# Two transformer blocks on one core: 32 copies of the bias rows, an earlier first weight split, and GpSimd's modulation units moved into the first mixer

## Time and profile before

| what | us |
|---|---|
| median of three runs (lowest, highest) | 928.85 (928.48, 933.09) |
| time of the profiled execution | 928.37 |
| its span, first to last instruction | 926.5 |
| PE busy | 864.4 (93%) |
| DVE busy | 593.9 (64%) |
| ACT busy | 481.2 (52%) |
| POOL busy | 306.3 (33%) |

### The profile page before, as it was taken

One profiled execution on the slowest core, in us unless ns is written; L12 is line 12 of the kernel. 1 busy time (PEld: TensorE's weight loads), 2 busy tenths in 40 slices (PEclk: granted clock), 3 DMA queues, 4 the chain that ended last, 5 costly groups with the idle time before them and its releaser, 6 DMA issues.

```text
span 926.5 us, 16135 instructions
## 1 busy us (share of the span) xinstructions
PE 864.4 (93%) x6742; PEld 836.8 (90%) x6742; DVE 593.9 (64%) x793; ACT 481.2 (52%) x740; POOL 306.3 (33%) x239
## 2 busy tenths in 40 slices
PE   4999999999799997969997979898999999999998
PEld 3899999988799997959997979898999999999998
DVE  4786454347789988586877685655556655546552
ACT  5755545444645653455342524433666666766641
POOL 1100000000699998646876755020153300000000
PEclk8999999999899999979998999999899999999999
DMA  7343597624456675425754454485355545343350
GB/s 258 122 157 132 58 156 164 139 78 174 162 197 227 259 255 211 175 110 205 272 203 155 188 204 160 137 280 182 115 219 192 195 138 182 129 145 137 137 204 23
DMA packets 28247, 158.42 MB, mean 171 GB/s; under 512 B 3456, under 2 KB 3984, under 8 KB 13840
## 3 DMA queue, kind: packets, MB, share of 16 engines
q1 hardware_dynamic: 24816, 146.37, 43.8%
q0 software_dynamic: 3360, 11.03, 7.4%
HBM read 150.04 MB, written 7.34 MB: 170 GB/s over the span
## 4 chain that ended last, share of the span: by engine, by line
PE 80%; DVE 10%; POOL 3%; ACT 3%; issue 2%; DMA 2%; SPq 0%; DVEq 0%; ACTq 0%; POOLq 0%
PE ps L451 78%; DVE wlo L1241 3%; PE ps L637 1%; ACT whi L879 1%; DMA arena<-positions 1%; PE ps L729 1%; DVE olo L1286 1%; DVE arena L1273 1%; DVE arena L1574 1%; DMA raw<-weights 1%; ACT L868 1%; DMA x<-x_t 1%; DVE hlo L1269 1%; POOL ada_ring L376 1%; DVE ohi L1284 0%
## 5 line engine op out<-in xcount | busy, mean ns | idle before, releaser
L1241 DVE TENSOR_TENSOR wlo<-raw,whi 128x1024 fp32r<-128x1024 f32 x224 | 316.1, 1451 | 155.1 <-ACT whi L879 155.1
L451 PE MATMUL ps<-hhi,whi 128*128 128x256 f32 x960 | 284.1, 296 | 32.1 <-DVE wlo L1241 15.6
L451 PE MATMUL ps<-hlo,whi 128*128 128x256 f32 x960 | 276.0, 288 | 0.0
L451 PE MATMUL ps<-hhi,wlo 128*128 128x256 f32 x960 | 275.8, 287 | 0.0
L879 ACT ACTIVATE whi<-raw 128x1024 fp32r<-128x1024 f32 x224 | 225.9, 1052 | 90.3 <-PE ps L451 68.9
L451 PEld LDWEIGHTS ps<-hhi,whi 128*128 128x128 f32 x960 | 188.7, 197 | 37.1 <-issue 36.5
L451 PEld LDWEIGHTS ps<-hlo,whi 128*128 128x128 f32 x960 | 189.0, 197 | 2.0 <-issue 1.9
L451 PEld LDWEIGHTS ps<-hhi,wlo 128*128 128x128 f32 x960 | 188.6, 196 | 0.0
L451 PE MATMUL ps<-ohi,whi 128*128 128x256 f32 x512 | 149.8, 293 | 12.6 <-DVE olo L1286 7.3
L376 POOL TENSOR_TENSOR ada_ring<-ada_ring,sil 128x1024 f32<-128x1024 f32 x48 | 105.7, 2201 | 140.4 <-DMA ada_ring<-ada 140.2
L451 PE MATMUL ps<-ohi,wlo 128*128 128x256 f32 x512 | 147.4, 288 | 0.0
(11 more groups left out here) (195 smaller groups left out, 1038.7 us busy)
## 6 DMA issues: line engine op xcount, KB each, us to landing
raw<-weights SPq DMA_DIRECT2D x112, 1024.0 KB, 5.1
ada_ring<-ada SPq DMA_DIRECT2D x48, 512.0 KB, 5.8
bias_rows_d<-ada_ring POOLq DMA_DIRECT2D x1, 4096.0 KB, 45.8
bias_rows_b<-fb POOLq DMA_DIRECT2D x1, 2048.0 KB, 88.5
arena<-bias_rows_d POOLq DMA_DIRECT2D x2, 1024.0 KB, 9.3
x<-x_t SPq DMA_DIRECT2D x2, 512.0 KB, 4.7
arena<-bias_rows_b POOLq DMA_DIRECT2D x1, 1024.0 KB, 7.4
arena<-bias_rows_d POOLq DMA_DIRECT2D x2, 512.0 KB, 13.1
```

The lines of the kernel that those rows point to most:

```text
L451: return pe.matmul(o, l, r, start=start, stop=stop, skip_group_check=skip)
L1241: dve.tensor_tensor(wlo[:, unit % UNITS, :, :], raw[:, c % RAW, 4 * half:4 * half + 4, :], whi[:, unit % UNITS, :, :].bitcast(F32), ALU.su ...
```

## The change

It has five parts.

1. `scr_d` and `scr_b` get 32 copies of a row instead of 128. They are read back in four DMAs of 32 partitions for each of two column ranges: eight instead of two for layer B, eight instead of four for layer D. `fb` and `fd` move out of their own tile and the ring into `early`, whose memory is later that of `ohi`; DVE therefore waits for the two writes before the norm of layer A's output.
2. At the start ACT calls `high(0)` before it works on the norm's sums, not after it. DVE splits the first half of chunk 0 before it waits for the norm and the second half after the third tile of the input, where both halves came after the first tile.
3. POOL runs the units 0 to 5 when the eight q and k convolutions are done, then the two bias writes, then the units 6 to 29. The loads of layer B's bias and the rope angles follow. The units 30 to 41 wait until layer B's inputs are ready (`h_ok_sem` 24), and 42 to 47 stay where they were. `ada_sum` holds 12 units.
4. SP loads the units 0 and 1 with chunk 11, 2 to 4 with chunk 12, three with each chunk from 13 to 19 (5 to 25), and one with each from 20 to 35 (26 to 41).
5. PE takes six units in each of the levels 2, 4 and 6 (through a turn of the banks 6 and 7), the units 18 to 23 after job 17, 24 to 29 after job 19, 30 to 35 after the jobs 28 to 33, 36 to 38 after job 35, and 39 to 41 after job 37. DVE takes the sums with `mod_of_slot` in the levels and with `take_mod` after that.

The diff, cut to what the prediction speaks of:

```diff
-        ada_sum = sb("ada_sum", [P, 6, P])
+        ada_sum = sb("ada_sum", [P, 12, P])
...
-        fb = sb("fb", [16, 512])
+        fb = early[0:16, 512:1024]
...
-        fd = ring[0:16, 0, 0:4, :].rearrange("p a b -> p (a b)")
+        fd = early[0:16, 0:512]
...
-                    if c == (JOB_B + 1 + u if u < 18 else JOB_C + (u - 18) if u < 42 else 76 + 2 * (u - 42)):
-                        if u < 2:
-                            sp.wait_ge(o_split_sem, 4)
-                            sp.wait_ge(scr_out_sem, 32)
-                        else:
+                    if c == ((11, 11, 12, 12, 12)[u] if u < 5 else 13 + (u - 5) // 3 if u < 26 else u - 6 if u < 42 else 76 + 2 * (u - 42)):
+                        if u >= 2:
                             sp.wait_ge(ada_mul_sem, u - 1)
...
+            pool.wait_ge(sil_ok_sem, 1)
+            pool.wait_ge(conv_ok_sem, 8)
+            for u in range(6):
+                ada_unit(u)
             pool.wait_ge(fd_ok_sem, 2)
             pool.wait_ge(nt_ok_sem, 4)
-            pool.dma_start(scr_d.rearrange("p h t -> h p t"), fd[:, :].unsqueeze(1).to_broadcast([16, P, 512])).then_inc(scr_out_sem, 16)
+            pool.dma_start(scr_d[0:32].rearrange("p h t -> h p t"), fd[:, :].unsqueeze(1).to_broadcast([16, 32, 512])).then_inc(scr_out_sem, 16)
             pool.wait_ge(bias_sb_sem, 1)
-            pool.dma_start(scr_b.rearrange("p h t -> h p t"), fb[0:8, :].unsqueeze(1).to_broadcast([8, P, 512])).then_inc(scr_out_sem, 16)
+            pool.dma_start(scr_b[0:32].rearrange("p h t -> h p t"), fb[0:8, :].unsqueeze(1).to_broadcast([8, 32, 512])).then_inc(scr_out_sem, 16)
+            for u in range(6, 30):
+                ada_unit(u)
             pool.wait_ge(scr_out_sem, 32)
             pool.wait_ge(o_split_sem, 4)
             bias_b = A(bias_at, 8, 384)
...
+            for a in range(0, P, 32):
+                pool.dma_start(bias_b[a:a + 32, :, 0:256], bass.AP(scr_b.tensor, 127 - a, [[8 * 512 - 1, 32], [512, 8], [1, 256]])).then_inc(bias_ok_sem, 16)
+                pool.dma_start(bias_b[a:a + 32, :, 256:384], bass.AP(scr_b.tensor, 255 - a, [[8 * 512 - 1, 32], [512, 8], [1, 128]])).then_inc(bias_ok_sem, 16)
...
-            pool.wait_ge(sil_ok_sem, 1)
-            for u in range(42):
+            pool.wait_ge(h_ok_sem, 24)
+            for u in range(30, 42):
                 ada_unit(u)
...
+                if lv in (2, 4, 6):
+
+                    b = taken(slot_of_mod(lv // 2 - 1))
+                    for u in range(3 * lv - 6, 3 * lv):
+                        ada(u, b)
                 parts(J, 0, 4)
...
             for J in range(JOB_OUT_A, JOB_B):
                 job(J, "T", ohi, olo, split=0 if J == JOB_OUT_A else None)
+                for u in {JOB_OUT_A + 1: range(18, 24), JOB_OUT_A + 3: range(24, 30)}.get(J, ()):
+                    ada(u)
...
-                if J >= 24:
-                    ada(J - 24)
+                for u in {35: (36, 37, 38)}.get(J, (J + 2,) if 28 <= J < 34 else ()):
+                    ada(u)
...
             act.wait_ge(ones_ok_sem, 6)
+            high(0)
             rsqrt(rs_a, S, 1.0 / D)
-            high(0)
...
+            low(0, range(1))
             next_rs()
-            prepare(0, lambda t: col("a_norm", t), None, hf_a, rs_a, hhi, hlo, between=lambda: low(0), after=0)
+            prepare(0, lambda t: col("a_norm", t), None, hf_a, rs_a, hhi, hlo, between=lambda: low(0, range(1, 2)), after=2)
...
+            dve.wait_ge(scr_out_sem, 32)
             for i in range(4):
...
-            dve.wait_ge(bias_ok_sem, 32)
-            attend(JOB_B, 4, 0, A(bias_at, 8, 384), False, {3: 1})
+            dve.wait_ge(bias_ok_sem, 128)
+            attend(JOB_B, 4, 0, A(bias_at, 8, 384), False, {})
```

More of the change, by code:

```diff
@@ L191, in slot, with slot_of_mod, slot_of_sum @@
             return ps[6 + k % 2], turn_free[k % 2], k // 2
+        turn_order = ["keys0", "keys1"]
+        for lv in range(1, LEVELS):
+            turn_order += [f"level{lv}_{g}" for g in range(4)]
+            turn_order += {1: ["values0"], 2: ["mod0"], 3: ["values1"], 4: ["values2", "mod1"], 5: ["values3"], 6: ["mod2"]}[lv]
+        turn_order += [f"sum{i}" for i in range(4)]
         def slot_of_level(lv, g):
-            return 2 + 4 * (lv - 1) + g + (0, 0, 1, 1, 2, 3, 4)[lv]
+            return turn_order.index(f"level{lv}_{g}")
         def slot_of_values(i):
-            return slot_of_level((1, 3, 4, 5)[i], 3) + 1
+            return turn_order.index(f"values{i}")
+        def slot_of_mod(i):
+            return turn_order.index(f"mod{i}")
+        def slot_of_sum(i):
+            return turn_order.index(f"sum{i}")
         def left_of(lv):
@@ L497, in sums, with ada @@
                 own_ss[0] += 1
-            def ada(u):
-                if u % 6 == 0:
-                    pe.wait_ge(mod_ok_sem, u // 6)
+            def ada(u, bank=ps[7]):
+                if u % 6 == 0 and u >= 24:
+                    pe.wait_ge(mod_ok_sem, u // 6 - 3)
                 pe.wait_ge(ada_mul_sem, u + 1)
-                mm(ps[7][:, u % 6:u % 6 + 1], ada_sum[:, u % 6, :], ones[:, 0:1], True, True).then_inc(ada_used_sem, 1)
+                mm(bank[:, u % 6:u % 6 + 1], ada_sum[:, u % 12, :], ones[:, 0:1], True, True).then_inc(ada_used_sem, 1)
             pe.wait_ge(ones_ok_sem, 6)
@@ L783, in _ @@
                     job(J, "T", ohi, olo)
-                if J < JOB_OUT_B + 3:
-                    ada(2 * J - 60)
-                    ada(2 * J - 59)
+                if J == JOB_OUT_B + 1:
+                    for u in range(39, 42):
+                        ada(u)
             x_sums(2)
@@ L803, in sums_c @@
                 sums(lambda t: sq4[:, t, :], 4, S, o_sq_sem, lambda t: h + 1)
-            def ada_c(J):
-                if J >= JOB_C + 3:
-                    ada(J - 25)
             for h in range(4):
@@ L829, in _ @@
                 job(J + 3, "T", hhi, hlo)
-                ada_c(J + 3)
                 job(J + 4, "S", hhi, hlo)
-                ada_c(J + 4)
                 job(J + 5, "S", hhi, hlo)
-                ada_c(J + 5)
-            def last_sums():
-                sums_c(3)
-                for u in range(39, 42):
-                    ada(u)
             mix_c(3)
@@ L842, in _ @@
                 if J == JOB_OUT_C:
-                    job(J, "T", ohi, olo, split=8, at={8: last_sums}, heads=4)
+                    job(J, "T", ohi, olo, split=8, at={8: lambda: sums_c(3)}, heads=4)
                 else:
@@ L1232, in _, with low @@
             rs_n = [0]
-            def low(c):
+            def low(c, halves=range(2)):
                 if c >= N_CHUNKS:
                     return
-                for half in range(2):
+                for half in halves:
                     unit = 2 * c + half
@@ L1408, in _ @@
                     take_values((1, 3, 4, 5).index(lv))
+                if lv in (2, 4):
+                    mod_of_slot(lv // 2 - 1)
                 for g in range(4):
@@ L1498, in attend @@
                         lows(J + 1)
-                    if not normed and i == 2:
-                        take_mod(0)
                     lows(J + 2)
@@ L1513, in attend @@
                         take_mod(modded[i])
+                    if not normed and i in (0, 3):
+                        take_mod(4 if i == 0 else 5)
                 scores_in(pairs - 1)
@@ L1544, in gains_of_c @@
             def gains_of_c():
-                take_mod(2)
-                dve.wait_ge(mod_ok_sem, 3)
+                for i in range(3):
+                    dve.wait_ge(slot(slot_of_mod(i))[1], slot(slot_of_mod(i))[2] + 1)
                 scaled_gain(0)
```

45 lines of the change are left out of this document (23 added, 22 removed).

## The result

The changed kernel takes **934.41 us** (median of 15 runs, 930.13 to 937.86) and the kernel before 928.73 us (15 runs beside them, 922.76 to 933.09). The ratio is 1.0054, 95% interval 1.0037 to 1.0070: it is slower by half a per cent. The forecast was 929.5 us with a range of 916 to 942.

A forecast was written before the change was run, and what follows sets the result against it. PE ends the time, so only its idle and slow stretches can be won. The terms -2.7 + 2 + 3 + 8 + 11 - 4 - 4 - 12.5 = +0.8 on the profiled 928.37 gave 929.2, as a median 929.5 us, range 916 to 942.

The forecast's parts named there:

- the trade that was forecast: Whole kernel: some 23 us of PE's waits won in layers B and C against 24 us lost in layer A.
- slower: Whole kernel: a time above the kernel before by more than about 0.5% (4.6 us), chance 0.31.
- within: Whole kernel: a time within about 0.5% (4.6 us) of the kernel before, chance 0.38.
- Start: PE's first job: splits of chunk 0 and ACT's high(0) leave the path to the first hlo, -2.7 us.
- Levels, first term: Way into layer A's levels: POOL's six first units slow two DVE splits and a small product, +2 us.
- Levels, second term: Layer A's levels: PE waits for POOL's units, unit 11 late in level 4, +3 us, bounds 0 and +12.
- The bias writes: Layer A's levels: writes take 22 us, slow the unit loads beside them, and POOL loses some 15 us.
- Output norm: Layer A's output norm: busy POOL slows twelve DVE operations by 0.7 us each, +8 us, bounds +4 and +13.
- After job 19: End of layer A: unit 29's load stands behind chunk 23 in SP's queue, PE waits, +11 us, bounds +7 and +14.
- Layers B and C: Waits shrink without POOL: -4 us at B's end, -4 at C's start, -12.5 at heads 2 and 3.
- The faster rival: Layer A hides the work: norm costs 4 us, levels 0, wait after job 19 8; 917.5 us, chance 0.30.
- The rival of a POOL that falls behind: Levels 4 and 6: POOL needs 6.6 us a unit, PE waits +12 us instead of +3; 940.5 us, chance 0.25.

The follow-up runs named there:

- ring29: The changed kernel with SP issuing the loads of units 26 to 29 earlier, with chunks 19 to 21 instead of 20 to 23: 925.49 us.
- start_only: The kernel before with only the second part of the change, the earlier split of chunk 0 at the start: 928.46 us, ratio 0.9981.
- norm_pause: The changed kernel with POOL waiting before unit 23 for the fourth split of layer A's output, so it rests in most of the norm: 936.51 us.
- copies128: The changed kernel with 128 copies of each bias row instead of 32, and the few wide reads of the kernel before: 974.31 us.
- write_early: The changed kernel with POOL issuing the two bias writes before unit 0, not between units 5 and 6: 927.55 us.
- combined_u4_nopause: combined_u4 with POOL resting only after unit 25, so units 24 and 25 may run during layer A's output norm: 922.55 us.
- combined_u4: combined with SP issuing the loads of units 26 to 41 later, with chunks 22 to 37 instead of 19 to 35: 917.30 us.
- combined: The changed kernel with ring29's loads, write_early's writes, units 0 to 2 alone first, POOL resting in layer A's norm, units 24 to 29 in layer B: 919.41 us.

## Why the prediction came out as it did

It is the trade that was forecast, and nearly all of its mechanisms are in the trace. 934.4 lies inside the range of 916 to 942, but just above the likeliest case's own 924 to 934. The sum said +0.8 us; the spans say +5.6 (926.5 to 932.1), and the medians +5.7. That is more than the 4.6 us that I had set as telling, so what came is "slower", to which I gave 0.31, and not "within", to which I gave 0.38. (0.8 on the median is 929.65, not 929.5, and the 23 us put down to B and C hold the 2.7 of the start.)

- **Start**: -2.7 forecast, -2.4 measured. What is won ahead of layer C seems to be kept now that POOL is idle there (ring29's 9.3 us at the start of layer B are 8.9 in the time, and its waits at heads 2 and 3 are again 2.30 and 2.37). In start_only, where POOL isn't idle, the gain did not reach the end.
- **Levels, first term**: +2 forecast, with bounds 0 and 4; **+6.7** measured, outside the bounds. This is the term that was most mis-sized. I counted "two times 0.77 and a small product"; four splits, four products and four two-column copies were slowed, by 7.2 us in all, and PE's idle time then cost it its clock, which I had not priced here though the earlier trace rows shows that price elsewhere. How much of it reaches PE varies: with the same code up to there, ring29 shows +6.6, norm_pause +2.75 and copies128 +1.1, the last two inside my bounds and with the transposes at the full clock. So the list of operations was too short in every trace, and part of the size of the miss is this trace's chance. The Trainium skill, GPSIMD Engine Reference, section 1, Specifications, names operations of VectorE in a 2-port mode among those that contend. The copy has one SBUF input and went from 166 to 1034 ns, which fits, though no trace here shows an operation's mode; I had applied the rule to the large operations only. write_early, in which POOL happens to rest there, shows PE's wait of 3.71 us back at 1.13 and the whole term gone.
- **Levels, second term**: +3 forecast, and +8.65 stands in the table. 2.12 us is the wait for unit 11, the wait that I had described. Part of the rest is PE's own additions. I wrote that they "only move from layers B and C to here: 0". That is true of the sum and wrong for the stages: the thirty units' additions are 60 matmuls and 8.2 us of PE's busy time in this trace, 4.7 of them in the levels (the distance of starts says somewhat less, 1.25 us for the six units of level 6). So the stages of layer A look that much dearer, and layers B and C that much cheaper. The third part is the clock, 0.83 of full speed over 160 to 180 us, behind the wait. These parts are read from the trace and not isolated: in norm_pause the wait for unit 11 is 0.23 us, and the stage still takes 10.8 us more than before.
- **The bias writes**: I took 22 us for them, by a quarter of 88.5; they took 12.3 and 21.8 us, and POOL lost 15.6 us behind them, where I had some 15. So close a match is partly luck, since some 4 us of it are the queue's order. By the fit in the Trainium skill, DMA: Bandwidth & Descriptors, section on the anatomy of one DMA on the SWDGE path (GpSimd's DMAs), an estimate has them land after 5.6 us; the measurement decides, and it is four times that.
- **Output norm**: +8 forecast, +7.15 measured; norm_pause and combined_u4_nopause show by two routes that the contention is the cause. Two errors offset each other in the size: I had four pairs at +2.1 us, and it was three at +2.4, since POOL stood still at the fourth.
- **After job 19**: +11 forecast, +11.45 measured, of which 2.1 are the additions of units 24 to 29, with the queue's order just as described, though the wait is two waits. ring29 removes them, and layer B then starts 9.3 us earlier. The other 2.65 us, of jobs 16 to 19, was not in my sum; the additions of units 18 to 23 are 1.4 us of it.
- **Layers B and C**: -20.5 forecast, -28.7 measured. The difference, 8.2 us, is about what the same 60 additions took there before the change (8.5 us of PE's busy time); that they are all of it is reckoned, not tested. At head 2 the wait fell by 5.29 and at head 3 by 3.22 us, against my 5.7 and 3.7.

The additions cancel between the halves. Without them layer A costs 28.4 against my 24. The way into the levels is +4.7 of that; the other terms missed by +0.95, -0.85, +1.25 and -1.65, which cancel by luck. The faster rival, that layer A hides its work, is refuted: the norm cost 7.15 us and not 4, and the levels nothing like 0. The rival of a POOL that falls behind was nearer than I allowed. Its place in the levels cost 2.12 us, not 12, but the four waits of norm_pause show that POOL had no slack after job 17.

What stays open: what write_early's gain of 8.6 us ahead of the norm owes to the quiet way into the levels and what to unit 11; why the way into the levels differs by up to 5.6 us between traces of the same code; and what makes DVE late for the waits that layer B has in combined_u4.

## What to carry to other kernels

When work moves to a helper engine in another stage, list every small operation of the engine that it contends with on the chain to the bottleneck, two-column copies too, and reckon with a slow restart of the bottleneck behind a new wait (here 3.68 us for sixteen transposes in place of 1.97). Look at more than one trace before you call a stage's size measured. In a queue that serves both the main stream and a side stream, the place of each side load decides: here four issue points were worth 1% of the time, and a helper that rested stalled the main stream until its loads were moved back (PE's wait of 6.44 us in combined, gone in combined_u4). A part of a change that is worth nothing alone (the 32 copies and their reads) may be what makes another one possible (40 us).

## What the runs showed of the hardware that I had not expected

- A DVE copy of 128 x 2 floats from SBUF to SBUF took 166 ns with POOL idle and 1034 ns in the mean of four (640 to 1850) beside POOL's products and sums.
- Two writes of 1 MB and 0.5 MB from 16 and 8 partitions took 12.3 and 21.8 us. A load of 512 KB that SP issued 8 to 12 us behind them landed so late that POOL idled for 15.59 us (unit 8 in the changed kernel) and 13.96 us (unit 2 in write_early). At four times the bytes the writes took 45.3 and 86.4 us (copies128). The smaller one, issued second, landed last in both.
